# Hybrid trunk kernel: entry reordered, x for the residual through the weight ring, first down digits ahead of the last hidden product

## What is computed

```python
def hyena_filters(L, ...):            # 64-wide sine network over positions, times a decay window
    h = sin(freq[0] * (feats @ w1 + b1)); h = sin(freq[1] * (h @ w2 + b2))
    return (h @ w3).reshape(L, 4, D) * exp(-t01 * abs(decay))
def hyena_branch(u, ...):
    v, x1, x2 = split(dwconv(u @ w_in + b_in), 3)
    z = x1 * long_conv(v, k[:, 0], k[:, 1], skip[0])
    z = x2 * long_conv(z, k[:, 2], k[:, 3], skip[1])
    return z @ w_out + b_out
# layer 0: u = x * (1 + scale1) + shift1;  scale, shift, gate = split(silu(c) @ mod_w + mod_b)
# x = LN(ALPHA * x + gate1 * hyena(u));  x = LN(ALPHA * x + gate2 * (silu(h @ w1) * (h @ w3)) @ w2)
# layer 1: RWKV-7 token mixer and top-2-of-8 experts (not touched by the change)
```

## Time and profile before

| | us |
|---|---|
| median of 3 runs | 2555.0 (2554.15 to 2557.62) |
| the profiled execution, its own time | 2555.83 |
| its span | 2554.0 |
| TensorE busy | 2424.6 |
| VectorE busy | 1621.3 |
| ScalarE busy | 1279.1 |
| GpSimd busy | 201.4 |

### The profile page before, as it was taken

The page is one execution under the profiler, slowest core; times in us unless marked ns, Lnnn a source line. Parts: engine busy times, 40 slices in busy tenths (PEclk is TensorE's granted clock), DMA queues, the critical chain, the costliest instruction groups (busy, mean ns, idle before and its releaser), DMA issues. The chain is left out here.

```text
span 2554.0 us, 48392 instructions
## 1 busy us (share of the span) xinstructions
PE 2424.6 (95%) x20546; PEld 1954.9 (77%) x20546; DVE 1621.3 (63%) x1790; ACT 1279.1 (50%) x1369; POOL 201.4 (8%) x182
## 2 busy tenths in 40 slices
PE   6999999899999799999999989999999999999996
PEld 2566666788778377777777869898989898888885
DVE  2543594422233854555556448888888888888887
ACT  3422013422222843444444347777777777777774
POOL 2000372100000020111111100000000000000000
PEclk9999999999999899999999999999999999999998
DMA  8378412233220211111101159999999999999992
GB/s 305 131 256 304 167 61 72 66 99 99 89 79 14 72 30 31 31 31 31 31 3 31 69 190 345 347 355 345 363 346 357 343 363 342 356 343 365 342 360 92
DMA packets 246230, 488.66 MB, mean 191 GB/s; under 512 B 13800, under 2 KB 104704, under 8 KB 245760
## 3 DMA queue, kind: packets, MB, share of 16 engines
q1 hardware_dynamic: 244894, 481.42, 53.4%
q10 hardware_dynamic: 1186, 5.01, 0.6%
HBM read 485.35 MB, written 1.05 MB: 190 GB/s over the span
## 5 line engine op out<-in xcount | busy, mean ns | idle before, releaser
L2730 DVE TENSOR_TENSOR w_low<-expert_w,w_high 128x1792 fp32r<-128x1792 f32 (+2 forms) x384 | 768.9, 2023 | 125.4 <-ACT w_high L1976 124.2
L1976 ACT CAST w_high<-expert_w 128x1792 fp32r<-128x1792 f32 (+2 forms) x384 | 652.8, 1701 | 247.1 <-PE bank L1466 154.4
L1466 PE MATMUL bank<-w_high,xg_high 128*128 128x448 f32 x1024 | 294.2, 369 | 4.0 <-DVE xg_low L2720 4.0
L1466 PE MATMUL bank<-w_low,xg_high 128*128 128x448 f32 x1024 | 291.8, 366 | 0.0
L1466 PE MATMUL bank<-w_high,xg_low 128*128 128x448 f32 x1024 | 291.5, 366 | 0.0
L1466 PEld LDWEIGHTS bank<-w_high,xg_high 128*128 128x128 f32 x1024 | 191.3, 189 | 20.1 <-DVE xg_low L2720 4.1
L1466 PEld LDWEIGHTS bank<-w_low,xg_high 128*128 128x128 f32 x1024 | 193.2, 189 | 15.5
L1466 PEld LDWEIGHTS bank<-w_high,xg_low 128*128 128x128 f32 x1024 | 193.0, 189 | 15.4
L1493 PE MATMUL bank<-w_high,hid_high 128*128 128x512 f32 x448 | 175.3, 391 | 0.0
L1493 PE MATMUL bank<-w_high,hid_low 128*128 128x512 f32 x448 | 174.5, 390 | 0.0
L1493 PE MATMUL bank<-w_low,hid_high 128*128 128x512 f32 x448 | 174.3, 389 | 0.0
(11 more groups left out here) (392 smaller groups left out, 4151.5 us busy)
## 6 DMA issues: line engine op xcount, KB each, us to landing
expert_w<-in_moe_w_dram SPq DMA_DIRECT2D x192, 1792.0 KB, 9.4
arena<-in_mod_w_dram SPq DMA_DIRECT2D x48, 1024.0 KB, 9.1
arena<-in_ffn_w_dram SPq DMA_DIRECT2D x44, 512.0 KB, 5.2
arena<-in_hy_w_in_dram SPq DMA_DIRECT2D x12, 1024.0 KB, 11.5
arena<-in_rw_w_rkv_dram SPq DMA_DIRECT2D x8, 1536.0 KB, 7.4
arena<-in_ffn_w_dram SPq DMA_DIRECT2D x11, 1024.0 KB, 4.9
arena<-in_hy_w_out_dram SPq DMA_DIRECT2D x4, 1024.0 KB, 8.9
arena<-in_rw_w_out_dram SPq DMA_DIRECT2D x1, 2560.0 KB, 13.8
```

The lines of the kernel that those rows point to most:

```text
L1466: last = pe.matmul(bank[b0 + v][:, 0:EH], x[:, k, :], w_[:, kk, v * EH:v * EH + EH], start=(k == 0 and x is XGH and w_ is wh), stop=(k == ...
L1976: act.copy(high_piece(kind, n), piece(kind, ering[q % ERN], n // 2, n % 2))\
L2730: dve.tensor_tensor(piece(kind, low[s], n // 2, n % 2), piece(kind, ering[s], n // 2, n % 2), high_piece(kind, n).bitcast(F32), ALU.subtract)\
```

## The change

- Entry: x is loaded into UT, u's home, instead of X2. On ScalarE's queue the filter weights and the skip row go ahead of the first decay load; the second decay load is issued after the first sine. ScalarE makes the second sine and windows(0) before any copy of x. TensorE makes filters(0) before it waits for x, then turns all eight tiles; the modulation chunks go in groups of 3, 2 and 3 behind spectra(0), behind spectra(1) and behind filters(3). The digits of the first two projection weights are made ahead of u's digits, on ScalarE between spectra(2) and spectra(3). TensorE's wait for the last spectrum copy goes to turn_v(0).
- Residual: x_again takes two slots of the weight ring, loaded ahead of hy_w_out, so ffn_start is 66 instead of 64. Tiles 0 to 3 are turned ahead of inverse(7) into banks 0 to 3 and scaled there by ScalarE, tiles 4 to 7 after m = 0 to 3.
- FFN: ScalarE's silu and VectorE's hid of the last hidden tile come behind the digits of c = 0, and the first down group takes m = 4 to 7 before it waits for hidden_taken.

```diff
@@ -415,10 +415,10 @@
...
         z_high, z_low = by_tile("z_high", work), by_tile("z_low", work + KT * T)
-        x_again = ZT
+        x_again = [ring[i].rearrange("p (t d) -> p t d", d=D) for i in range(2)]
...
         rows = KSP[:, 0:1, 0:512].rearrange("p a (r c) -> p (a r) c", c=P)
-        xin = X2.rearrange("p a b -> p (a b)").rearrange("p (a b) -> p a b", b=D)
+        xin = UT.rearrange("p a b -> p (a b)").rearrange("p (a b) -> p a b", b=D)
@@ -580,7 +580,7 @@
...
-        ffn_start = 24 + 12 + 24 + 4
+        ffn_start = 24 + 12 + 24 + 2 + 4
@@ -704,11 +704,12 @@
...
                     load_mod(0, c)
+            for i, name in enumerate(("ctx", "x")):
+                s = ld.slot_to_load((sem("x_again"), KT))
+                assert s == i
+                sp.dma_start(x_again[i], a[name][0].rearrange("(t p) d -> p t d", p=P)).then_inc(w_loaded[s], 16)
...
                 load_cols(a["hy_w_out"], c, "out_full")
-            sp.wait_ge(sem("bins_full"), 16)
-            load("ld_x_again", x_again[:, 0:2, :], a["ctx"][0].rearrange("(t p) d -> p t d", p=P))
-            load("ld_x_again", x_again[:, 2:4, :], a["x"][0].rearrange("(t p) d -> p t d", p=P))
@@ -842,9 +843,6 @@
...
-            pe.wait_ge(sem("ld_common"), 16)
-            pe.wait_ge(sem("ld_x"), 32)
@@ -853,37 +851,35 @@
...
-            turn_x(0, 4)
...
             filters(0)
-            turn_x(4, KT)
+            pe.wait_ge(sem("ld_common"), 16)
+            pe.wait_ge(sem("ld_x"), 32)
+            turn_x(0, KT)
...
             last.then_inc(sem("rows_turned"), 1)
-            pe.wait_ge(sem("silu_ready"), 1)
-            pe.wait_ge(sem("x_taken"), KT)
-            mod_chunk(0, 0)
-            mod_chunk(0, 1)
             filters(1)
-            mod_chunk(0, 2)
...
             spectra(0)
+            pe.wait_ge(sem("silu_ready"), 1)
+            pe.wait_ge(sem("x_taken"), KT)
+            for c in range(3):
+                mod_chunk(0, c)
+            filters(2)
+            spectra(1)
...
             mod_chunk(0, 4)
-            filters(2)
-            mod_chunk(0, 5)
-            spectra(1)
-            mod_chunk(0, 6)
-            mod_chunk(0, 7)
             filters(3)
+            for c in range(5, EARLY):
+                mod_chunk(0, c)
...
             spectra(3)
-            pe.wait_ge(sem("spectrum_taken"), 16)
@@ -898,6 +894,8 @@
...
                 pe.wait_ge(sem("conv_done"), m + 1)
+                if m == 0:
+                    pe.wait_ge(sem("spectrum_taken"), 16)
@@ -977,11 +975,27 @@
...
                 inverse(g - 1)
...
+            def turn_x_again(k):
+                b = k if k < 4 else 6 + k % 2
+                if k >= 6:
+                    pe.wait_ge(sem("x_scaled1"), k - 1)
+                for t in range(NB):
+                    last = pe.transpose(bank[b][:, t * P:(t + 1) * P], x_again[t // 2][:, t % 2, k * P:(k + 1) * P], ident)
+                last.then_inc(sem("x_again"), 1)
...
+            for i in range(2):
+                rg.loaded_slot()
+            pe.wait_ge(sem("bins_taken"), 16)
+            for k in range(4):
+                turn_x_again(k)
...
                     s = rg.loaded_slot()
+                if m < 4:
+                    pe.wait_ge(sem("x_scaled1"), m + 1)
@@ -994,13 +1008,8 @@
...
                 last.then_inc(sem("out_full"), 1)
-                if m == 0:
-                    pe.wait_ge(sem("ld_x_again"), 32)
-                if m >= 2:
-                    pe.wait_ge(sem("x_scaled1"), m - 1)
-                for t in range(NB):
-                    last = pe.transpose(bank[6 + m % 2][:, t * P:(t + 1) * P], x_again[:, t, m * P:(m + 1) * P], ident)
-                last.then_inc(sem("x_again"), 1)
+                if m < 4:
+                    turn_x_again(4 + m)
@@ -1025,14 +1034,14 @@
...
             rg.read_loop(FT, hidden)
-            pe.wait_ge(sem("hidden_taken"), FT + 2)
...
                 for g in range(2):
-                    for m in range(KT):
+                    for m in (4, 5, 6, 7, 0, 1, 2, 3) if c + g == 0 else range(KT):
+                        if c + g == 0 and m == 0:
+                            pe.wait_ge(sem("hidden_taken"), FT + 2)
@@ -1556,11 +1565,10 @@
...
                               decay[:, 2 * n * D:(2 * n + 2) * D].partition_broadcast(P)).then_inc(sem(f"ld_decay{n}"), 16)
+            load("ld_filter", w3[0:HY_W, :], a["hy_f_w3"])
+            load("ld_filter", skip[0:1, :], a["hy_skip"].rearrange("a (o b) -> o (a b)", o=1))
             load_decay(0)
-            load("ld_filter", skip[0:1, :], a["hy_skip"].rearrange("a (o b) -> o (a b)", o=1))
-            load("ld_filter", w3[0:HY_W, :], a["hy_f_w3"])
             load("ld_table0", arena[:, table:feats_at], consts[1][:, 0:feats_at - table])
-            load_decay(1)
@@ -1611,40 +1619,44 @@
...
             sine(0)
+            load_decay(1)
             rates(0)
-            copy_x(0, 3)
...
             windows(0)
-            copy_x(3, KT)
+            copy_x(0, KT)
...
             copy_spectra(0)
-            take_mod(0, 0)
...
             copy_spectra(1)
-            take_mod(0, 1)
+            take_mod(0, 0)
...
             windows(3)
+            take_mod(0, 1)
...
+            def loaded(n):
...
+            def in_high(m):
...
             copy_spectra(2)
+            act.wait_ge(sem("filter_taken"), 8)
+            in_high(0)
+            in_high(1)
...
-            def loaded(n):
...
-            def in_high(m):
@@ -1652,9 +1664,6 @@
...
                 act.copy(out_high[m % 2], w).then_inc(sem("out_high"), 1)
...
-            in_high(0)
-            in_high(1)
@@ -1705,6 +1714,15 @@
...
                 return s
+            def scale_x(k):
+                act.wait_ge(sem("folded"), 1)
+                act.wait_ge(sem("x_again"), k + 1)
+                b = bank[k if k < 4 else 6 + k % 2]
+                for s in range(2):
+                    last = act.activation(XT[:, k, seg[s]], b[:, seg[s]], ACT.Identity,
+                                          bias=per_stream(gate_bias, k, s), scale=float(ALPHA))
+                last.then_inc(sem("x_scaled1"), 1)
@@ -1712,13 +1730,11 @@
...
                     out_w_high(1)
-            act.wait_ge(sem("folded"), 1)
+                    for x in range(4):
+                        scale_x(x)
             for m in range(KT):
-                act.wait_ge(sem("x_again"), m + 1)
-                for s in range(2):
-                    last = act.activation(XT[:, m, seg[s]], bank[6 + m % 2][:, seg[s]], ACT.Identity,
-                                          bias=per_stream(gate_bias, m, s), scale=float(ALPHA))
-                last.then_inc(sem("x_scaled1"), 1)
+                if m < 4:
+                    scale_x(4 + m)
@@ -1743,8 +1759,9 @@
...
             rw.read_loop(FT - 1, lambda f: silu(f, upper(f + 1) - 1 - ffn_start))
-            silu(FT - 1, FT - 1)
             for c in range(FT // 2):
+                if c == 1:
+                    silu(FT - 1, FT - 1)
@@ -2252,11 +2269,6 @@
...
                 last.then_inc(sem("u_new"), 1)
-            for k in range(KT):
-                dve.wait_ge(sem("u_in_high"), k + 1)
-                dve.tensor_tensor(u_in_low[k], UT[:, k, :], u_in_high[k].bitcast(F32), ALU.subtract)\
-                    .then_inc(sem("u_in_low"), 1)
@@ -2266,6 +2278,13 @@
...
+            in_low(0)
+            in_low(1)
+            for k in range(KT):
+                dve.wait_ge(sem("u_in_high"), k + 1)
+                dve.tensor_tensor(u_in_low[k], UT[:, k, :], u_in_high[k].bitcast(F32), ALU.subtract)\
+                    .then_inc(sem("u_in_low"), 1)
@@ -2282,8 +2301,6 @@
...
-            in_low(0)
-            in_low(1)
@@ -2414,8 +2431,9 @@
...
             with_loop(dve, FT - 1, lambda f, j: (lower(f + 1, j + 1), hid(f, j)))
-            hid(FT - 1, FT - 1)
             for c in range(FT // 2):
+                if c == 1:
+                    hid(FT - 1, FT - 1)
...
```

More of the change, by code:

```diff
@@ L1625, in _ @@
             copy_spectra(1)
-            take_mod(0, 1)
+            take_mod(0, 0)
             rates(3)
             windows(3)
-            copy_spectra(2)
-            for o in range(4):
-                copy_spectra(3, [o])
-                for k in (2 * o, 2 * o + 1):
-                    act.wait_ge(sem("u_new"), k + 1)
-                    act.copy(u_in_high[k], UT[:, k, :]).then_inc(sem("u_in_high"), 1)
+            take_mod(0, 1)
             def loaded(n):
@@ L1646, in in_high @@
                 act.copy(proj_high[m % 2], w).then_inc(sem("proj_high"), 1)
+            copy_spectra(2)
+            act.wait_ge(sem("filter_taken"), 8)
+            in_high(0)
+            in_high(1)
+            for o in range(4):
+                copy_spectra(3, [o])
+                for k in (2 * o, 2 * o + 1):
+                    act.wait_ge(sem("u_new"), k + 1)
+                    act.copy(u_in_high[k], UT[:, k, :]).then_inc(sem("u_in_high"), 1)
             def out_w_high(m):
```

## The result

The changed kernel took 2533.9 us (median of 4 runs, 2530.8 to 2534.8) against 2556.3 for the kernel before beside it (4 runs): 0.9909 of its time, 95% interval 0.9892 to 0.9926. The forecast was 2532.0, range 2527 to 2542. The profiled execution has a span of 2533.0, so 21.0 less than that of before, where the forecast's sum says 23.0.

A forecast was written before the change was run, and what follows sets the result against it. TensorE, busy 2424.6 of 2554.0 us, was taken as the bound, so only its idle or half-clock time could be won. Terms 6.9 + 2.4 + 1.3 + 1.3 + 2.1 + 6.2 + 2.8 = 23.0 took median 2555.0 to 2532.0, range 2527 to 2542.

The forecast's parts named there:

- First projection matmul, 81.7: Entry: the first projection matmul starts at 81.7 instead of 88.6 us, a gain of 6.9 us.
- I leave x where it is: Entry: x still lands at 25.9 us, 21.6 after its issue, despite the reordered loads.
- filters 0 behind x: Entry, sign of being wrong: filters 0 come later than x; 3 us later would lose those 3 us.
- the last link at spectra(0): Entry: GpSimd's four sums end at 37.3, after TensorE's own work at 36.5, so spectra(0) start at 37.4, not 43.48.
- The half clock at the projection, 2.4: Projection start: without idle time the clock holds, 12 matmuls in 2.8 instead of 5.25 us, a gain of 2.4 us.
- I count all of it.: Projection: loads follow matmuls by a distance, not an absolute time, so the entry's whole gain is passed on.
- Last inverse, 2.1: Last inverse: 2.5 us idle remain, the clock holds, output projection begins at 383.15 instead of 385.22: 2.1 us.
- The rival in which the clock falls all the same: Last inverse: the clock falls despite the turned tiles, costing 2.1 us, total 2534; chance 0.28.
- Transposing sets and last residual, 1.3 + 1.3: Output projection: three transpose sets between groups go, 1.3 us; tile 7's residual no longer waits for transposes and scaling, 1.3 us.
- Down, 6.2 + 2.8: First down matmul: at 699.35 instead of 705.54, 6.2 us; 15 matmuls at 0.234 instead of 0.427, 2.8 us.
- late operand: Rival: the first down group waits for another operand, a weight or digit buffer; part 3 fails, 2541 us; chance 0.07.
- FFN tile 0, the way to be slower: Rival: FFN tile 0, loaded late (issue about 409), holds ScalarE in the output projection; 2560 us, chance 0.02.

The follow-up runs named there:

- after_third: The changed kernel itself, with no further edit, profiled and timed a third time: 2532.9 us.
- e4: Kernel before with only the first two projection weights' digits made early and TensorE's wait for the last spectrum copy moved to turn_v(0): 2550.1 us (0.9979).
- e3_down: Kernel before with only the FFN part: last silu and product behind the digits of c = 0, m = 4 to 7 first: 2546.6 us (0.9970).

## Why the prediction came out right, and where not

The total came out 2 us above the forecast, and every part of the change paid. Term by term, with filters 0 and the transposes of x in after_third first, which the first point needs:

```profile
18.78 7.19 PE L828 MATMUL bank<-arena 64*128 64x512 f32 x8 [7.57 <-ACT arena L1582]
25.90 6.19 PE L851 MATMUL bank<-arena 128*128 128x128 f32 x32
```

- *First projection matmul, 81.7.* It came at 80.4 in the first profile, at 81.3 and 83.1 in the other two. "I leave x where it is" failed in all three: x landed at 24.6 to 24.9 instead of 25.9. So it did in all nine traces with the reordered entry (24.5 to 24.9, against 25.8 to 26.6 in the other four); which part of the order does it was not tried. Decay was there at 15.7 in the first profile (I took 16), and filters 0 ended ahead of x, at half clock. In the other two it was there only at 17.3, filters 0 ended at 25.9, and x waited for them for 1 us; I had named filters 0 behind x as a sign of being wrong. GpSimd was the last link at spectra(0) as said, and nothing on VectorE took the place of the digits: low digits done at 78.0, I had said 78.9. Of the 1.3 us won beyond the forecast in the first profile, 0.6 are the earlier x (spectra at 36.8 instead of 37.4) and 0.6 an error of the sum: I put 14.0 us for spectra(2, 3), the length of their row, but the next matmul starts 13.4 behind their start (66.96 to 80.37). What I did not price is the half clock behind GpSimd's wait: I looked for it only at the 4 to 6 us waits and entered 7.06 us for spectra(0). That is 0 to 3.1 us, most often 1.4 to 1.7.
- *The half clock at the projection, 2.4.* Gone; the lead rises by 2.1, from 8.2 to 10.3. The 0.3 less is the second matmul, 0.63 us behind the first instead of 0.23.
- *"I count all of it."* This is the step that failed, by 3.8 us in the first profile. The argument behind it was right: a load follows a matmul by a distance, and the waits did not grow. It left out that the waits of 2 to 3 us, which the projection has anyway, can be followed by half clock, in one execution and not in the next; what decides it is open. Two stretches cost 3.1; what is left, 0.7 to 0.9 around tile 11, only the first of the three profiles has (from the copy of tile 10 to that of tile 11 it is 10.6 us there and 9.5 to 10.4 in all other traces), and I don't know its cause.
- *Last inverse, 2.1.* From its start to the output projection 7.17 us became 5.05: 2.1. The rival in which the clock falls all the same had a chance of 0.28 and did not come in any of eight traces. The rule of the Trainium skill (TensorE: Matmul & The Clock Gate, Part 4: PE-mode transpose) that transposes don't count as busy as matmuls do would have had it so; in this gap the traces disagree with it (3.84 us behind turned tiles, 5.2 to 6.7 without). At the entry they are on both sides: transposes alone were followed by filters at full clock in before (3.70) and at half clock in e4 (7.19).
- *Transposing sets and last residual, 1.3 + 1.3.* From the first output matmul to the last residual 48.6 us (385.2 to 433.8) became 45.9: 2.7. The residual starts 0.12 us behind its group's end, by the matmul's row at 421.94 + 0.39.
- *Down, 6.2 + 2.8.* e3_down alone has 6.2, and in the changed kernel the lead grows by 2.7 from the first down matmul to layer 1, where the clock stays high. The chance of 0.07 for a late operand did not come in.
- *FFN tile 0, the way to be slower.* The load was issued at 400.6, as I had it (409 on the old clock, less a lead of 8.6), and the tile was cast at 407.06, directly behind out_w_high without idle time. ScalarE had 3.7 us of idle time ahead of those casts.

That the time came within 2 us of the forecast is in part luck, as errors of both signs met: 1.3 more at the entry and 0.9 at the FFN's start against 3.8 lost in the projection. What layer 1 adds is of the same kind: its part from its beginning to the first expert matmul, which the change does not touch, took 673.1, 669.7 and 669.5 us in the three profiles of the changed kernel and 671.8 in before.

## What to carry to other kernels

When a wait is removed upstream, ask of the short waits downstream not only whether they grow but whether TensorE's clock holds behind them. Here that differed between kernels and between executions of one kernel, by some 1.5 us a time, and a single trace shows one draw of it. Work without a deadline, such as transposes for a later step, is best put where TensorE waits some 4 us: it took two us of idle time and with it the fall of the clock. And when a buffer moves to another home, go through the waits that guarded the old one: the one left on GpSimd cost 2.6 us, give or take 1.9.

## What the runs showed of the hardware that I had not expected

- Idle times of 1.67 us, not only of 4 and more, were followed by the 1.2 GHz level, in five traces of seven, and the same wait of the same kernel once with and once without.
- The first rise of the clock came at different times in executions that do the same until then: filters 0 behind the first transposes of x took 3.70 us in before and 7.19 in e4_digits, where the whole entry then lies 4.9 us later. This is as large as most single edits here, and may be a good part of the 13 us over which the timed runs of before lie; no run here ties it to them.
